# Two-layer decoder trunk: the reciprocal root of every RMSNorm, and where TensorE sums and spreads it

## The reference

```python
def rmsnorm(x, g):
    xf = x.astype(jnp.float32)
    y = xf * lax.rsqrt(jnp.mean(xf * xf, axis=-1, keepdims=True) + RMS_EPS)
    return (y * g.astype(jnp.float32)).astype(x.dtype)

def swiglu(x, w_in, w_out):
    gate, up = jnp.split(x @ w_in, 2, axis=-1)
    return (jax.nn.silu(gate) * up) @ w_out

for l in range(DEPTH):                                   # DEPTH = 2
    g = norm_g[l]
    h = h + 0.5 * rmsnorm(swiglu(rmsnorm(h, g[FFN1_PRE]), ffn_w_in[l, 0], ffn_w_out[l, 0]), g[FFN1_POST])
    hn = rmsnorm(h, g[MIX_PRE])
    u_pool, q, k, v, gate_pool, gate_attn = jnp.split(hn @ w_in[l], SPLITS, axis=-1)
    y_pool = pool_mixer(u_pool, pool_w_grp[l], pool_scale[l], w_pool_proj[l])
    y_attn = swa_attention(q, k, v, sinks[l]) @ w_attn_proj[l]      # shapes left out
    merged = jax.nn.sigmoid(gate_pool) * y_pool + jax.nn.sigmoid(gate_attn) * y_attn
    h = h + rmsnorm(merged @ w_o[l], g[MIX_POST])
    h = h + 0.5 * rmsnorm(swiglu(rmsnorm(h, g[FFN2_PRE]), ffn_w_in[l, 1], ffn_w_out[l, 1]), g[FFN2_POST])
```

## Time and profile before

| | |
|---|---|
| three runs | 1256.12, 1258.23, 1259.37 us; median 1258.23 |
| the profiled execution | 1260.2 us, of it 1258.1 us span of the core |
| mean granted clock of TensorE | 0.991 of full speed |
| busy share of the span | PE 98%, DVE 59%, ACT 42%, POOL 36% |
| chain that ended last | PE 75%, issue 8%, DVE 7%, ACT 4%, POOL 3%, DMA 1% |
| PE idle ahead of line 480 | 9.4 us in 10 waits for POOL's `rt` (line 1320) |

### The profile page before, as it was taken

One profiled execution on the slowest core, in us unless ns is written; L12 is line 12 of the kernel. 1 busy time (PEld: TensorE's weight loads), 2 busy tenths in 40 slices (PEclk: granted clock), 3 DMA queues, 4 the chain that ended last, 5 costly groups with the idle time before them and its releaser, 6 DMA issues.

```text
span 1258.1 us, 25020 instructions
## 1 busy us (share of the span) xinstructions
PE 1228.3 (98%) x9813; PEld 1201.1 (95%) x9813; DVE 738.5 (59%) x1021; ACT 528.4 (42%) x736; POOL 452.7 (36%) x529
## 2 busy tenths in 40 slices
PE   6999999999999999999999999999999999999998
PEld 5999999899999999999999999998989998999997
DVE  4655544658866575544466555447578757655443
ACT  5333334535654443333343332344366544443331
POOL 2655410304512355452026455003054122666301
PEclk9999999999999999999999999999999999999999
DMA  8555356453256365544636553573624653654440
GB/s 280 185 174 168 114 172 207 121 183 123 70 135 201 101 200 168 167 137 139 218 103 205 181 164 118 166 230 96 197 95 102 187 164 110 211 185 152 156 141 33
DMA packets 203138, 196.87 MB, mean 156 GB/s; under 512 B 4168, under 2 KB 202032, under 8 KB 203072
## 3 DMA queue, kind: packets, MB, share of 16 engines
q1 hardware_dynamic: 202784, 195.69, 49.9%
q10 hardware_dynamic: 288, 0.27, 0.1%
HBM read 194.90 MB, written 1.05 MB: 156 GB/s over the span
## 4 chain that ended last, share of the span: by engine, by line
PE 75%; issue 8%; DVE 7%; ACT 4%; POOL 3%; DMA 1%; SPq 0%; POOLq 0%; ACTq 0%
PE bank L398 24%; PE bank L400 24%; PE bank L399 23%; ACT w_hi L721 2%; DVE w_lo L914 2%; POOL rt L1320 2%; POOL acc L1316 1%; PE bank L480 1%; DMA raw<-in_ffn_w_in 1%; DVE h L995 1%; DVE x_lo L965 1%; DVE tmp L986 1%; DVE s L1135 1%; POOL acc L1313 1%; DVE stats L1139 1%
## 5 line engine op out<-in xcount | busy, mean ns | idle before, releaser
L398 PE MATMUL bank<-x_hi,w_hi 128*128 128x272 f32 (+1 forms) x2048 | 596.5, 291 | 6.1 <-DVE w_lo L914 4.4
L914 DVE TENSOR_TENSOR w_lo<-raw,w_hi 128x2048 fp32r<-128x2048 f32 (+2 forms) x205 | 426.1, 2083 | 289.1 <-ACT w_hi L721 289.1
L400 PE MATMUL bank<-x_hi,w_lo 128*128 128x272 f32 (+1 forms) x2048 | 589.6, 288 | 0.0
L399 PE MATMUL bank<-x_lo,w_hi 128*128 128x272 f32 (+1 forms) x2048 | 587.9, 287 | 0.0
L721 ACT ACTIVATE w_hi<-raw 128x2048 fp32r<-128x2048 f32 (+2 forms) x216 | 357.3, 1659 | 496.1 <-PE bank L400 495.5
L398 PEld LDWEIGHTS bank<-x_hi,w_hi 128*128 128x128 f32 x2048 | 388.5, 190 | 10.1 <-DVE w_lo L914 4.8
L399 PEld LDWEIGHTS bank<-x_lo,w_hi 128*128 128x128 f32 x2048 | 388.5, 190 | 0.3
L400 PEld LDWEIGHTS bank<-x_hi,w_lo 128*128 128x128 f32 x2048 | 388.4, 190 | 0.0
L398 PE MATMUL bank<-hid_hi,w_hi 128*128 128x272 f32 (+1 forms) x704 | 201.5, 286 | 0.0
L399 PE MATMUL bank<-hid_lo,w_hi 128*128 128x272 f32 (+1 forms) x704 | 201.3, 286 | 0.0
L400 PE MATMUL bank<-hid_hi,w_lo 128*128 128x272 f32 (+1 forms) x704 | 200.9, 285 | 0.0
(11 more groups left out here) (157 smaller groups left out, 1124.5 us busy)
## 6 DMA issues: line engine op xcount, KB each, us to landing
raw<-in_ffn_w_in SPq DMA_DIRECT2D x88, 1024.0 KB, 5.1
raw<-in_ffn_w_out SPq DMA_DIRECT2D x32, 768.0 KB, 4.4
raw<-in_w_in SPq DMA_DIRECT2D x24, 1024.0 KB, 5.4
raw<-in_ffn_w_out SPq DMA_DIRECT2D x32, 640.0 KB, 4.0
raw<-in_w_in SPq DMA_DIRECT2D x16, 512.0 KB, 5.2
raw<-in_w_attn_proj SPq DMA_DIRECT2D x32, 256.0 KB, 4.4
raw<-in_w_o SPq DMA_DIRECT2D x8, 1024.0 KB, 5.8
raw<-in_w_pool_proj SPq DMA_DIRECT2D x8, 512.0 KB, 3.4
```

The costliest lines, as they stand in the source:

```text
L398: pe.matmul(ps[:, t0:T], w[0], a_hi[:, t0:T], start=start, stop=False)
L399: pe.matmul(ps[:, t0:T], w[0], a_lo[:, t0:T], start=False, stop=False)
L400: return pe.matmul(ps[:, t0:T], w[1], a_hi[:, t0:T], start=False, stop=stop)
L914: last = dve.tensor_tensor(lo, w, hi.bitcast(F32), ALU.subtract)
```

## The change

- `sum_part` takes the place of `sum_squares`: for a pre-norm one part, since GpSimd now adds all eight squares (ADDS 7 for a pre-norm, 5 for a post-norm); for a post-norm three parts, two of which stand among the last products (ahead of the last tile and ahead of its last k; behind W_o both ahead of the last k). The third group of tokens is now the last 128, so all are 128 wide.
- `spread_rms` uses transposes. For a pre-norm it stands between the two tiles of the unit behind the first pair, and the sum behind the whole pair.
- The first pair's k = 0 starts with its eight products of `x_hi` once that is there.
- A post-norm's root: ACT takes the square root of the sums (`take_root`), DVE the reciprocal and one Newton step (`post_rms`). The table of Sqrt is loaded behind the last Silu of an FFN and ahead of the W_o units, that of Silu behind a pre-norm of an FFN.
- On DVE the split that stood around `boundary` is made whole ahead of the last output tile; the split of the second next unit (`u0 + 4`, or 42) stands ahead of `take_rms`.
- The loops over the units of the FFN's second matrix, and the first four units of its first, are written out in TensorE's list. `keep_warm` behind a post-norm's spread: 5 for 8.

```diff
@@ norm on TensorE
-            def sum_squares(q, l):
+            def sum_part(q, l, part):
...
-                for part in range(3):
...
+                for b, first in enumerate(TOKENS):
+                    last = pe.matmul(small[:, S_SUM + b:S_SUM + b + 1], src[:, first:first + P], ones[:, 0:1],
...
             def spread_rms(q, l):
                 pe.wait_ge(rt_ready, l * NORMS + q + 1)
-                    last = pe.matmul(small[:, S_BC + b * P:S_BC + b * P + n], rt[0:n, b:b + 1].to_broadcast([n, P]),
-                                     ident[0:n, 0:n], start=True, stop=True)
+                    last = pe.transpose(small[:, S_BC + first:S_BC + first + P], rt[:, b:b + 1].to_broadcast([P, P]),
+                                        ident[:, :])
...
-                spread_rms(4 * f, l)
+                sum_part(4 * f, l, 0)
+                for j, (banks, lag) in enumerate(in_turn):
+                    unit(u0 + 2 + j, l, tile0 + 4 + 2 * j, banks, lag, KD, x_hi, x_lo, t0=t0,
+                         between=(lambda: spread_rms(4 * f, l)) if j == 0 else None)
...
+                        if u == N_OUT - 1 and mt == 1:
+                            sum_part(4 * f + 1, l, 0)
...
+                            if u == N_OUT - 1 and mt == 1 and kk == KF - 1:
+                                sum_part(4 * f + 1, l, 1)
...
-                sum_squares(4 * f + 1, l)
+                sum_part(4 * f + 1, l, 2)
                 keep_warm(WARM_RMS)
@@ ScalarE
+            def take_root(n):
+
+                act.wait_ge(ssq_done, n + 2)
+                act.activation(root[:, 0:3], small[:, S_SUM:S_SUM + 3], ACT.Sqrt, scale=1.0 / D, bias=eps[:, 0:1]
+                               ).then_inc(root_done, 1)
...
                 pre_norm(l * NORMS + 4, g_cur[:, 4 * KD:5 * KD], l * 3 * KD + 2 * KD)
+                act.preload_act_table(ACT.Silu)
@@ VectorE
+            def post_rms(q, l):
+
+                n = l * 3 + q // 2
+                dve.wait_ge(root_done, n + 1)
+                dve.tensor_scalar(var[:, 0:3], small[:, S_SUM:S_SUM + 3], 1.0 / D, EPS, ALU.mult, ALU.add)
+                dve.reciprocal(near[:, 0:3], root[:, 0:3]).then_inc(newton, 1)
...
                 split_lo_between(u0 + 3, l, lambda: mean_square(4 * f, l))
+                split_lo(u0 + 4, l)
                 take_rms(4 * f, l)
                 take_gate(f, l, 0)
-                split_lo(u0 + 4, l)
...
-                    take_out(3)
-                    mean_square(1, l)
-                    split_lo_between(U_Q, l, lambda: boundary(0, l, l * 4 * KD + KD, g_cur[:, 2 * KD:3 * KD]))
+                    take_out(3, between=lambda: split_lo(U_Q, l))
+                    post_rms(1, l)
+                    boundary(0, l, l * 4 * KD + KD, g_cur[:, 2 * KD:3 * KD])
...
                 split_lo(41, l)
+                split_lo(42, l)
                 take_rms(2, l)
...
-WARM_RMS, WARM_X = 5, 8
+WARM_RMS, WARM_X = 5, 5
```

More of the change, by code:

```diff
@@ L493, in ffn @@
                     else:
-                        deep_pair(*first_pair)
+                        deep_pair(*first_pair, high_ready=high_ready)
                 else:
-                    deep_pair(*first_pair, t0=t0)
-                spread_rms(4 * f, l)
-                with pe.Fori(0, (N_IN - 2) // 4) as i:
-                    for j in range(4):
-                        banks, lag = (((4, 5), FFN_LAG), ((2, 3), 4), ((0, 1), FFN_LAG), ((2, 3), 4))[j]
-                        unit(u0 + 2 + j, l, tile0 + 4 + 2 * j, banks, lag, KD, x_hi, x_lo, i * 4, i * 8, t0)
@@ new lines, in ffn @@
+                u0, tile0 = U_FFN_OUT[f], T_FFN_OUT[f]
+                for u in range(N_OUT):
+                    pair, j = u // 4 % 2, u % 4
+                    unit_split(u0 + u, l)
+                    pe.wait_ge(hid_ready, l * 2 * KF + f * KF + OUT_K0[j] + OUT_K[j])
+                    for mt in range(2):
+                        if j == 0:
+                            tile_free(tile0 + u // 4 * 2 + mt, l, 4)
+                        if u == N_OUT - 1 and mt == 1:
+                            sum_part(4 * f + 1, l, 0)
+                        for k in range(OUT_K[j]):
+                            kk = OUT_K0[j] + k
+                            if u == N_OUT - 1 and mt == 1 and kk == KF - 1:
+                                sum_part(4 * f + 1, l, 1)
+                            last = products(bank[2 * pair + mt], weights(u0 + u, k, mt), hid_hi[:, kk, :],
+                                            hid_lo[:, kk, :], kk == 0, kk == KF - 1, t0)
+                        if mt == 0 and j == 3:
+                            last.then_inc(first_done, 1)
+                    last.then_inc(unit_done, 1)
@@ L615, in after_kv @@
                 for n in range(4):
-                    unit(U_Q + n, l, T_Q + 2 * n, Q_BANKS[n], (8, 6, 4, 4)[n], KD, x_hi, x_lo, t0=t0)
+                    unit(U_Q + n, l, T_Q + 2 * n, Q_BANKS[n], (8, 6, 4, 4)[n], KD, x_hi, x_lo, t0=t0,
+                         between=(lambda: spread_rms(2, l)) if n == 0 else None)
                     if n == 2:
@@ L768, in ffn @@
                         silus(f, l, (j - 1) // 2)
+                act.preload_act_table(ACT.Sqrt)
                 u0 = U_FFN_OUT[f]
@@ L881, in _ @@
                 merge_hi(7, l)
-                act.preload_act_table(ACT.Silu)
+                act.preload_act_table(ACT.Sqrt)
                 split_hi(65, l)
@@ L1308, in add_squares @@
             def add_squares(q, l):
-                for m in range(1, KD - 2):
+                for m in range(1, ADDS[q % 2] + 1):
                     pool.wait_ge(sq_done, (l * NORMS + q) * KD + m + 1)
```

157 lines of the change are left out of this document (94 added, 63 removed).

## The result

| | before | changed |
|---|---|---|
| runs beside each other, median | 1258.80 us (4) | 1238.41 us (4; 1236.76 to 1240.17) |
| span of the profiled execution | 1258.1 us | 1235.5 us |

The ratio is 0.9835, with an interval of 0.9819 to 0.9850: 20.4 us less, where 5 had been forecast. The time lies in the forecast's range of 1230 to 1259 only because that had been widened down to the first rival (1232); of the forecast case's own 1249 to 1259 it is well clear.

A forecast was written before the change was run, and what follows sets the result against it. TensorE, busy 98% of the span, was taken as the bound. Pre-norms 6.1 us (waits included) plus post-norms 3.3 less clock 4.0 gave 5.4 off 1258.2: forecast 1253, range 1230 to 1259.

The forecast's parts named there:

- the first rival: At the pre-norms GpSimd takes the port between two DVE splits, so waits and their half-clock spells go: 1232 us, chance 0.13.
- the forecast case: GpSimd's pre-norm power is held until DVE's splits end, TensorE waits, half clock follows: 1249 to 1259 us, chance 0.80.
- The wait for GpSimd: At pre-norms GpSimd's power waits for DVE's row of splits; TensorE idles 1.3, 2.6 twice and 2.05 three times, in us.
- The clock: Half-clock spells behind the pre-norm waits: five charged at 8.5 us against 4.5 before, a loss of 4.0.
- Pre-norm without waits: At each pre-norm, 1.05 us of TensorE stay off product, for 4.7 (mixer), 3.6 (FFN) and 4.9 (first) before.
- Post-norm: At post-norms, last product's slot to spread's end takes 4.5 for 5.17 us; 3.3 us gained over the six.
- Early start: First pair's k = 0 starts on x_hi 0.54 us sooner, but k = 1 waits for its x_lo: costed at nothing.
- fillers: Eight fillers made five behind a post-norm's spread are hidden in the wait for x_lo: nothing.
- table loads: Sqrt's table load stands where ScalarE waits for TensorE anyway: no cost.
- The longer list: TensorE's written-out list, 6946 rows for 5264, might make it wait for instructions: more than 1262 us, chance 0.04.

The follow-up runs named there:

- the pre-norm part alone: Changed kernel with root, sums, fillers and table loads of the post-norms as before the change; split's move and early start kept: 1230.58 us, ratio 0.9764.

## Why the prediction was wrong, point by point

- **The wait for GpSimd: wrong, and it decided the case.** The step that failed is "GpSimd gets in when DVE's row of splits ends, not between two of them". The two rows under it were read rightly. What failed was to carry them over: one of them stands behind an operation on 16 partitions, which was in the rows of before and in the diff (it goes when the third group becomes 128 wide), and which I took for a matter of 0.07 us. With it put back, the forecast's durations are met: 5.19 us in the mixer (6.25 - 0.85 = 5.4 was worked out), 3.98 in the FFNs (4.1), waits of 13.3 together (12.65).
- **The first rival was right** in that GpSimd gets in between two splits, and had 0.13. By the Trainium skill, SBUF — State Buffer, section "SBUF: two separate sides", the lock is held "for the whole instruction"; the changed kernel's rows agree with that in the power's end, 0.72 behind the first piece, and the rows with an operation on 16 or 64 partitions ahead do not. Nor is DVE blocked in return by the power: its last 0.72 run beside the second piece, and the row of four takes 4.62 with GpSimd inside it and 4.61 with GpSimd kept out. The rival's 1232 is 6 too low: 1.2 of it in the pre-norms and 1.3 in the post-norms, which it shares with the forecast, 1.4 at the start, and 2.2 by which the two profiles lie further apart than the medians.
- **The clock: right in size.** Six places with waits had five more spells than the changed kernel (7 for 2), all five at pre-norms, and 1.7 each fits the spans. That half clock stays away where the waits do was said too. The number of spells is less sure than this sounds: it differs between profiles of one kernel (last section).
- **Pre-norm without waits: right.** 1.05 off product had been forecast; the pair's sum takes 0.59 of TensorE's list (240.53 to 241.12) and the transposes 0.25 (244.21 to 244.46). The forecast's gain without waits would have been 3.85 + 2 x 3.65 + 3 x 2.55 = 18.8, and 4.5 of the clock: 23.3. The table shows 22.1.
- **Post-norm: right at the FFNs (0.8 for 0.7), wrong behind W_o** (-0.7 and 0.2), where the sums ahead of the last k wait for GpSimd (0.20 and 0.94) and half clock comes as it did before. The step that failed is the assumption that all six look like the one in the earlier trace rows: 2.0 for 3.3. And it was credited to the wrong edit. With the split moved, the root by ScalarE is worth nothing (3.28 for 3.26); the split's move shortens the power by 0.9; and the sums' placement, which the text charged with 0.8 a time and let pass, costs 7 us (1230.93 without it). Within the changed kernel the terms came out: the root lasts 0.26 (0.28 had been taken), and the spread starts 4.04 behind the last product's slot (4.0).
- **Early start, fillers, table loads: right,** nothing. The longer list was not run by itself; the trace has no wait for it.

## What to carry to other kernels

Where GpSimd must get in between DVE operations on SBUF, look at every DVE operation ahead of them, not only at the long ones: one on 16 or 64 partitions in place of 128 made GpSimd's small operation last up to 5.2 us here instead of 1.8. Making small work full width (here the last 128 tokens instead of the last 16) can be worth more than the work. Sums moved ahead of the last products were paid in full here; behind the last product they lie beside the square that has to be awaited anyway. And test the parts of a change apart: here the pre-norm part with the move of the split gave 28 us, and the other edits of the post-norm took 8 back.

## What the runs showed of the hardware that I had not expected

- With a DVE operation on 16 or on 64 partitions ahead of a row of DVE splits (two SBUF inputs each) with no gap, GpSimd's power is held out until the row ends: 1.78 becomes 2.91 (two pieces), 3.99 (a half and a whole split), 5.19 (four pieces). The same operation on 128 partitions doesn't. It need not be the last one ahead of the row. Six kernels with it and nine without, on both sides of the change, agree. Whether it acts by itself or by the few nanoseconds that the power then starts earlier, how long the effect lasts, and what ends it besides a gap, was not tried.
- DVE does not pay when GpSimd gets in: four pieces take 4.62 us with the power inside and 4.61 without. And GpSimd's memsets, which read nothing, are not held by the splits: in the run with fourteen of them ahead of the power each lasts 0.177 to 0.184 us.
- The operation on few partitions is not the only condition. Near the start of the program an add of GpSimd is held to the end of the second split in both kernels (3.44 us in the changed one) with no such operation ahead. Why stays open.
- Spells of half clock came in different numbers in two profiles of one kernel: two in one profile of the changed kernel, four in another; none and two in those of the pre-norm part alone. A few us of a single profile can't be read.
